# A fused two-block transformer kernel: six edits of instruction order and of who does what, on ScalarE, VectorE, TensorE and GpSimd

## The reference

```python
def first_block(x, p, ...):
    h = rmsnorm(x, attn_pre_g[i])
    proj = h @ w_in[i]                      # queries, six kinds of keys and values, gates
    (q_n, kc, vc, ksl, vsl, kwn, vwn, g_n, q_s, k_s, v_s) = jnp.split(proj, IN_SPLIT_POINTS, axis=-1)
    ...
    mix = jnp.concatenate([o_nsa, o_swa], axis=-1) @ w_o[i]
    x = x + rmsnorm(mix, attn_post_g[i])
    h = rmsnorm(x, mlp_pre_g[i])
    a, u = jnp.split(h @ w_gate_up[i], [D_FF], axis=-1)
    a = causal_dwconv(a, conv_w[i], conv_b[i])
    y = (jax.nn.gelu(a, approximate=True) * u) @ w_down[i]
    x = x + rmsnorm(y, mlp_post_g[i])
    e = p[i] @ w_ple[i]
    x = x + e * jax.nn.sigmoid(x @ w_ple_gate[i])

def second_block(x, c, ctx, c_ctx, ...):
    for i in range(DEPTH_2):                # two layers
        h = rms_norm(x, pre_g[i]) * (1.0 + scale) + shift
        hc = rms_norm(xc, pre_g[i]) * (1.0 + cscale) + cshift
        # layer 0: differential attention, 8 heads of 2 x 64; layer 1: grouped queries, 8 heads of 128, 2 of keys
        y, yc = mixer(h, hc, w_in, w_out[i], ...)
        x = x + gate * rms_norm(y, post_g[i])
        xc = xc + cgate * rms_norm(yc, post_g[i])   # layer 0 only
```

## Time and profile before

| | us |
|---|---|
| median of 3 runs | 1668.63 |
| lowest and highest | 1667.78, 1669.62 |
| the profiled execution | 1671.54 |
| its span in the trace | 1670.2 |
| mean granted TensorE clock | 0.976 of full |

### The profile page before, as it was taken

How to read it: one execution, slowest core, us unless ns; L and a number is a source line. 1 busy time by engine, 2 the same in 40 slices (tenths; PEclk the granted TensorE clock), 3 DMA queues, 4 the chain that set the end, 5 groups by cost and what they waited for, 6 DMA issues and landing times. The chain is left out here.

```text
span 1670.2 us, 21955 instructions
## 1 busy us (share of the span) xinstructions
PE 1563.2 (94%) x7933; PEld 1294.0 (77%) x7933; DVE 1059.8 (63%) x2146; ACT 612.8 (37%) x1496; POOL 719.2 (43%) x676
## 2 busy tenths in 40 slices
PE   5899799999999999999999999999997989899997
PEld 4786444688877787877798999899985767898886
DVE  7646666457777767748866565665666468656544
ACT  3213656242122220113443544444345255344431
POOL 6856000328678648685544124412444304423330
PEclk9998999999999999999999999999998999999999
DMA  6623000315444436553321011101111411111221
GB/s 181 187 80 91 11 1 1 127 64 150 122 139 133 120 107 215 176 189 115 120 64 39 14 50 51 46 18 39 51 51 51 151 64 51 52 50 39 64 89 51
DMA packets 115884, 142.58 MB, mean 85 GB/s; under 512 B 11048, under 2 KB 75200, under 8 KB 115776
## 3 DMA queue, kind: packets, MB, share of 16 engines
q1 hardware_dynamic: 89968, 91.77, 18.1%
q10 hardware_dynamic: 25808, 49.40, 9.1%
HBM read 132.74 MB, written 8.40 MB: 85 GB/s over the span
## 5 line engine op out<-in xcount | busy, mean ns | idle before, releaser
L470 POOL TENSOR_SCALAR w_hi<-w_raw 128x512 fp32r<-128x512 f32 x316 | 247.2, 782 | 667.4 <-PE ps L485 510.7
L472 POOL TENSOR_TENSOR w_lo<-w_raw,w_hi 128x512 fp32r<-128x512 f32 x316 | 440.3, 1393 | 26.4
L483 PE MATMUL ps<-w_hi,h_hi 128*128 128x384 f32 (+2 forms) x768 | 281.1, 366 | 4.1 <-DVE x L2596 1.8
L484 PE MATMUL ps<-w_lo,h_hi 128*128 128x384 f32 (+2 forms) x768 | 267.5, 348 | 0.0
L485 PE MATMUL ps<-w_hi,h_lo 128*128 128x384 f32 (+2 forms) x768 | 266.9, 348 | 0.0
L483 PE MATMUL ps<-h_hi,w_hi 128*128 128x512 f32 (+1 forms) x616 | 246.4, 400 | 8.0 <-POOL w_lo L472 4.2
L485 PE MATMUL ps<-h_hi,w_lo 128*128 128x512 f32 (+1 forms) x616 | 239.0, 388 | 0.0
L484 PE MATMUL ps<-h_lo,w_hi 128*128 128x512 f32 (+1 forms) x616 | 238.8, 388 | 0.0
L2541 DVE SCALAR_TENSOR_TENSOR mod_acc<-mod_piece,csil,mod_acc 128x512 f32<-128x512 f32 x140 | 158.5, 1171 | 27.0 <-DMA mod_piece<-in_ada_w 22.9
L483 PEld LDWEIGHTS ps<-w_hi,h_hi 128*128 128x128 f32 x768 | 147.0, 191 | 16.0 <-DVE x L2596 2.5
L484 PEld LDWEIGHTS ps<-w_lo,h_hi 128*128 128x128 f32 x768 | 147.2, 192 | 9.7 <-issue 0.5
(11 more groups left out here) (323 smaller groups left out, 2789.3 us busy)
## 6 DMA issues: line engine op xcount, KB each, us to landing
mod_piece<-in_ada_w ACTq DMA_DIRECT2D x96, 256.0 KB, 3.2
w_raw<-in_w_gate_up SPq DMA_DIRECT2D x88, 256.0 KB, 3.2
w_raw<-in_a_w_in SPq DMA_DIRECT2D x128, 128.0 KB, 2.3
w_raw<-in_w_down SPq DMA_DIRECT2D x22, 512.0 KB, 4.0
w_raw<-in_b_w_in SPq DMA_DIRECT2D x20, 512.0 KB, 3.6
w_raw<-in_w_out SPq DMA_DIRECT2D x16, 512.0 KB, 3.8
w_raw<-in_w_in SPq DMA_DIRECT2D x8, 512.0 KB, 4.2
w_raw<-in_w_o SPq DMA_DIRECT2D x8, 512.0 KB, 3.8
```

The lines of the kernel that those rows point to most:

```text
L470: pool.tensor_scalar(hi[:, e, :], raw[:, e, :], 1.0, 0.0, ALU.mult, ALU.add).then_inc(*s["pool_step"].up())
L472: m = pool.tensor_tensor(lo[:, e, :], raw[:, e, :], hi[:, e, :], ALU.subtract)
L483: pe.matmul(out, a[0], b[0], start=start, stop=False)
L484: pe.matmul(out, a[0], b[1], start=False, stop=False)
```

## The change

Six edits, from the start of the program to its end.

1. **Second weight tile.** The tile kv1 is named in `BY_SCALAR`. ScalarE writes its high halves, one ACTIVATE of a whole pair each (128 x 1024), ahead of its copies of the keys; GpSimd does the low halves alone.
2. **Quads.** TensorE multiplies a turned chunk with the values one turn later than before, across quads. ScalarE copies the next turned chunk before it takes the exponentials of the slots ahead. VectorE scales the next quad's p before it writes the outputs of the quad before.
3. **Projection out.** The scaling of the row goes from ScalarE to VectorE, and for the last row the root and the scaling stand ahead of the low half of the row before.
4. **Down.** The three loads of the residual move in ScalarE's queue behind the 16 loads of modulation pieces.
5. **out0.** The turn of row t-2, not t-3, stands in ScalarE's list at tile t; squares of y come first for every tile behind the first; the row's write to memory comes one tile later, and the loads of the tables at tile 3, not 2. VectorE has the same y-first order, and the query tables one tile later.
6. **Held split.** GpSimd's split of z8,0 waits for the inverse roots of q8 (`rms`, ("q8", 0)) instead of the context's rotated keys.

The diff, cut to its core:

```diff
+BY_SCALAR = ("kv", 1)
...
                 if tile == ("z8", 0):
-                    pool.wait_ge(*s["roped8"].at(("kv8", TX + 1)))
+                    pool.wait_ge(*s["rms"].at(("q8", 0)))
+            if tile == BY_SCALAR:
+                pool.wait_ge(*s["act_step"].at(("w_hi", q)))
             for e in range(2):
-                pool.tensor_scalar(hi[:, e, :], raw[:, e, :], 1.0, 0.0, ALU.mult, ALU.add).then_inc(*s["pool_step"].up())
-                pool.wait_ge(*s["pool_step"].now())
+                if tile != BY_SCALAR:
+                    pool.tensor_scalar(hi[:, e, :], raw[:, e, :], 1.0, 0.0, ALU.mult, ALU.add).then_inc(*s["pool_step"].up())
+                    pool.wait_ge(*s["pool_step"].now())
                 m = pool.tensor_tensor(lo[:, e, :], raw[:, e, :], hi[:, e, :], ALU.subtract)
...
+    before = None
     for q in qs:
         ahead = slots_behind(qs, q.n)
-        for i in range(len(q.chunks) + 1):
-            if i < len(q.chunks):
-                pe_quad_turn(k, pe, qs, q, i)
+        for i in range(len(q.chunks)):
+            pe_quad_turn(k, pe, qs, q, i)
             for slot in ahead[2 * i:2 * i + 2]:
                 pe_slot_scores(k, pe, qs, slot)
-            if i > 0:
-                pe_quad_values(k, pe, qs, q, i - 1)
+            if before is not None:
+                pe_quad_values(k, pe, qs, *before)
+            before = q, i
+    pe_quad_values(k, pe, qs, *before)
...
     def turn_out(t):
-        pe.wait_ge(*s["scaled"].at(("out1", t)))
+        pe.wait_ge(*s["dve_step"].at(("out1", t)))
...
+    for q in range(0, KD, 2):
+        pair = (KD + q) // 2
+        act.wait_ge(*s[f"w_loaded{pair % 2}"].at(pair))
+        act.activation(k.place(BY_SCALAR)[0][:, q:q + 2, :], k.w_raw[:, pair % 2, :, :], ACT.Copy, scale=1.0).then_inc(*s["act_step"].up(("w_hi", q)))
     for j in range(3):
...
     for q in qs:
-        ahead = slots_behind(qs, q.n)
-        for i in range(len(q.chunks) + 1):
-            if i < len(q.chunks):
-                act_quad_copy(k, act, qs, q, i)
+        ahead, last = slots_behind(qs, q.n), len(q.chunks) - 1
+        for i in range(last + 1):
+            act_quad_copy(k, act, qs, q, i)
+            for slot in (ahead[2 * i - 2:2 * i] if i > 0 else []):
+                act_slot_exp(k, act, qs, slot)
+            if i == last:
+                for slot in ahead[2 * i:2 * i + 2]:
+                    act_slot_exp(k, act, qs, slot)
             if i == 0 and q.n > 0 and qs[q.n - 1].kind > 0:
                 outputs(qs[q.n - 1])
-            for slot in ahead[2 * i:2 * i + 2]:
-                act_slot_exp(k, act, qs, slot)
...
     next(k.down_loads)
     act.dma_start(k.post4[:, :], k.row(k.ins["mlp_post_g"])).then_inc(*s["post4_in"].up("all", 16))
-    for t in range(TX - 1):
-        act.dma_start(k.x4(t), k.x_dram[:, t, :]).then_inc(*s[f"x4_in{t}"].up("x", 16))
...
     loads(KD - 1 + KD + 1)
+    for t in range(TX - 1):
+        act.dma_start(k.x4(t), k.x_dram[:, t, :]).then_inc(*s[f"x4_in{t}"].up("x", 16))
...
     for t in range(TA):
-        if t >= 3:
-            turn_out(t - 3)
-        act_add(k, act, "y3", t, k.x7, k.y7[:, t % 2, :], OUT0_BANKS[t % 3], rows, ("out0", t, 1), None, y_first=t == 1)
-        if t == 2:
-            act.wait_ge(*s["x_out"].at(("7", 1)))
+        act_add(k, act, "y3", t, k.x7, k.y7[:, t % 2, :], OUT0_BANKS[t % 3], rows, ("out0", t, 1), y_first=t > 0)
+        if 1 <= t <= TX:
+            act.wait_ge(*s["added"].at(("y3", t - 1)))
+            act.dma_start(k.x_dram[:, t - 1, :], k.x7[:, t - 1, :]).then_inc(*s["x_out"].up(("7", t - 1), 16))
+        if t >= 2:
+            turn_out(t - 2)
+        if t == 3:
+            act.wait_ge(*s["x_out"].at(("7", 2)))
             act.dma_start(k.cosb[:, :, :], k.ins["cos_b"]).then_inc(*s["tabb_in"].up("all", 16))
...
         for slot in slots_behind(qs, q.n):
             dve_slot_least(k, dve, qs, slot)
+        if q.n + 1 < len(qs):
+            dve_quad_scale(k, dve, qs, qs[q.n + 1])
         if q.n > 0 and qs[q.n - 1].kind > 0:
             outputs(qs[q.n - 1])
-        if q.n + 1 < len(qs):
-            dve_quad_scale(k, dve, qs, qs[q.n + 1])
...
     dve.wait_ge(*s["rms"].at((tag, t)))
-    if tag == "y3" and before:
-        dve_scale_row(k, dve, t - 1)
+    if before:
+        dve_scale_row(k, dve, tag, t - 1)
...
+    dve_last(k, dve, "y1", TX - 1)
+    dve.wait_ge(*s["rms"].at(("y1", "x", TX - 1)))
+    dve_scale_row(k, dve, "y1", TX - 1)
     turn_out(TX - 2)
-    dve_last(k, dve, "y1", TX - 1)
     turn_out(TX - 1)
```

More of the change, by code:

```diff
@@ L1769, in act_project_out, with act_add @@
     turn_out(TX - 2)
[L1770 removed]
     turn_out(TX - 1)
[L1774 removed]
+def act_add(k, act, tag, t, x, yt, banks, rows, prod, y_first=False):
     s = k.sig
@@ L1795, in act_add @@
         row_squares()
-    if before and scaled is not None:
-        act.wait_ge(*s["rms"].at((tag, t)))
-        act_scale(k, act, rows(t - 1), x[:, t - 1, :], 2 * t + 1, (scaled, t - 1))
 def act_last_squares(k, act, tag, t, x, rows):
```

28 lines of the change are left out of this document (9 added, 19 removed).

## The result

| | before | after |
|---|---|---|
| median of the runs | 1668.2 (4 runs) | 1646.1 (4 runs, 1644.2 to 1647.2) |
| the profiled execution | 1671.54 | 1645.49 |
| its span | 1670.2 | 1644.2 |
| mean granted clock | 0.976 | 0.980 |

The ratio after to before is 0.9865, with a 95% interval of 0.9851 to 0.9880: 22.1 us faster by the medians, where 24.6 was forecast. The two profiled executions differ by 26.0.

A forecast was written before the change was run, and what follows sets the result against it. TensorE, busy 94% of the span, was taken to bound the kernel. Six terms, 1.8 + 6 + 2.2 + 2.0 + 8.4 + 4.2 = 24.6, took the median from 1668.6 to 1644 us, range 1633 to 1656.

The forecast's parts named there:

- A: Second weight tile at the start: ScalarE writes high halves, loads become the bound, ready near 56.8; 1.8 us gained.
- B: Quads: TensorE's 14.0 us of waits for the turned copy go; 6 us gained, a little under half.
- first rival: Quads gain nothing, the wait moving from the copy to the scaled p or the exponentials; 1650 us, chance 0.18.
- the sign given for that rival: Quads: a group of TensorE waits for the exponentials or for p with over 8 means the gain-nothing rival holds.
- C: Projection out of block one, last row: root and scaling come earlier, so the last turn does; 2.2 us gained.
- D: Down's first weights no longer share queues with the residual's loads; 2.0 us gained, two thirds of 2.94.
- up to the 2.94 comes back: Down: step claiming GpSimd's 2.94 wait for the first w_down pair is recovered at most, of which 2.0 was taken.
- E: out0: row turns no longer stand behind a sum in ScalarE's queue; waits and half clock go, 8.4 us gained.
- F: Split of z8's first tile held until q8's roots: VectorE's roots and rotations no longer stretched; 4.2 us gained.
- third rival: Held split is paid later, stretching VectorE's small operations in four units of scores, about 1 each; 1648 us, chance 0.06.
- second rival: Full clock comes back too where waits go, behind the start, down, quads and q8's roots: 8.5 more, 1636 us, chance 0.12.
- fourth: Rival: ScalarE's later exponentials lengthen the score loop, 1.9 for each of 24 quads, 45 lost; 1695 us, chance 0.04.

The follow-up runs named there:

- either half of B alone: Changed kernel with only TensorE's deferral of the quads' edit, 1649.5 us; with only ScalarE's and VectorE's halves of it, 1645.0 us.
- B put back: Changed kernel with the quads' order of before on TensorE, ScalarE and VectorE: 1654.3 us, ratio 0.9916.
- C and D put back: Two runs: changed kernel with projection out's row scaling and root order of before, 1648.0 us; with the residual's loads ahead of down's first weights, 1649.5 us.

## Why the prediction was right, and where it was wrong

**A** was right as a mechanism (1.06 per high half, loads the bound, last low half at 56.99 for 56.8). Its size is 2.2 for 1.8 at the wait, and the runs don't contradict it. The first pair's 3.2 has a share of clock.

**B** forecast 6, and the first pair shows 5.0. Of this 3.1 is shown to be B's, and the half-clock stretch at 209 (1.6) may be. The weak step is "the wait for the copy then goes by construction, because a turn of 0.66 and up to two scores lie between": it goes, but either half of B alone takes most of it (14.5 to 2.6 or 2.2), and the two together leave more waits for the scaled p than either, most likely since the deferral takes away what covered the scaling. The prediction saw the scaling as next in line, with 2.1 of slack read from one turn, and its first rival named it. By the sign given for that rival (waits for p of over 8), it holds as a mechanism, since they are 13.7, though not in its price, since the stage gains. I had priced the three halves of B as one.

**C** was right in size, 2.2 in the first pair and 1.7 put back, but in part by luck. The forecast is made of waits alone; TensorE's idle time shows 0.9 to 1.4, and the rest came from a half clock for which it had no term.

**D** was wrong, and the first pair of traces hid it: 2.7 in down less 0.6 in gate look like the forecast 2.0. The failed step is "up to the 2.94 comes back". The load is earlier, but GpSimd splits beside VectorE's sums at 1.06 and 1.60 per chunk, and TensorE catches up with it one part later; the wait moves from 3.71 and 0.60 to 1.27 and 2.82. The prediction named the earlier sums and gave them a third of the price. On the kernel before, nothing of the 2.94 is left in 12 runs (at most 1.2 of it).

**E** was right in place, waits and clock: 8.4 forecast, 8.5 in the first pair, 8.4 put back. Replaying three queues from the durations paid off here.

**F** was right: 4.2 forecast, 4.2 in both ways, and 2.5 to 3.0 against the one further trace with the old hold. The roots took 2.4 for 5.1. Of the third rival one wait of 1.06 came true, not four: VectorE's blocked operation, a scaling of p (1.42 for 0.62), is off the path in the units, and on it only ahead of the rotation. The 4.2 has this 1.06 in it, so the rest gave back 5.3. By the durations that is the roots' 2.7, as priced, and 2.4 from the four rotations, priced at 1.5: they took 1.46, 0.76, 0.88 and 0.96 before and take 0.42 now. The rule of the Trainium skill that the prediction named (page "SBUF — State Buffer", section "SBUF: two separate sides") is borne out in its direction: beside the moved split the rotation at 1417.71 takes 1.35 where it took 0.42. Its cost here is small.

**The sum.** With the stages' own numbers A 2.2, B 3.1, C 1.7 to 2.2, D 0, E 8.4 and F 4.2 are about 20, and the medians show 22.1. The forecast of 24.6 is high by B (3, or 1 to 2 if the half-clock stretch at 209 is B's) and D (2). What lies between 20 and 22 is within the interval of the ratio (20.0 to 24.9). The first pair's 26.0 is more than the medians' 22.1 because the profiled execution of before lay 3.3 above its median and that of after 0.6 below its own. So the total is less far off than two of its terms: A, E, F and C's size came out near, and the rest is within the noise. The range's upper end, 1656, is 2.5 wider than the prediction's own sum gives (1644 and half of 19). The **second rival**, the full clock coming back by 8.5, didn't happen as a whole: the clock went from 0.976 to 0.980 or 0.982. The **fourth** (the score loop grows) didn't happen with the three lists together; the 5.7 that the deferral costs on top of the other two is a loss in the same loop, but it came with waits for the scaled p, and the share of the later exponentials in it isn't separated.

The best of what ran is the changed kernel with TensorE's deferral left out: 1645.0 us and ratio 0.9851 (0.9835 to 0.9868), below the changed kernel's 0.9865 and 0.9874, but with overlapping intervals. In the stage itself the difference is plain, 195.60 against 201.3, though from one trace of it against seven.

## What to carry to other kernels

When an edit reorders several engines' lists around one wait, run each engine's half alone: here one half gave 8.8 us of its stage, and the other took 5.7 of it back. Look not only at what a moved instruction waits for, but at what it had covered where it stood. When a wait goes from the table, read the duration of the group behind it, too, for the wait can have moved inside. And don't take a stage's gain from one pair of traces if it is about as large as a low-clock stretch costs: put the edit back, or make it alone, and read the waits.

## What the runs showed of the hardware

Most of the scatter of this program is the clock's. Some stretches repeated to 0.1 or 0.3 us (quads 201.30 to 201.38 in seven executions, heads 484.84 to 485.16 in fourteen), while down, one unchanged list of instructions, took 134.64 and 144.78 at granted 0.99 and 0.93. In the second execution the two stretches at half clock in down (10.2 us each) came right behind waits of 2.54 and 2.22; in the first, a wait of 2.82 at the same place was followed by a shorter one. In the quads, the same wait of 1.09 was followed by 3.4 us at half clock in before, and by none with B put back. So a wait of the same length doesn't always cost the same clock, and I can't say from these runs what decides it.

Nor does the same time at half clock always cost the same. In the beginning of the quads it lasted 17.1 to 23.9 us in those seven executions, and their stage differed by 0.08: TensorE has waits for VectorE there (0.4 to 2.7 each), and by 182 the traces with 23.9 (C and D put back) are back within 0.1 of the changed kernel's, though 1.9 and 2.3 behind it at 151. The 3.4 us at 209 in before, on four matmuls that ran without a gap, cost 1.6 and weren't made good.
